# Attention in a two-layer diffusion block: maxima one pair per step, sums by wide matmuls, shift rows by DMA, and one addition moved from GpSimd to VectorE

## The reference

```python
def block_attention(q, k, v, scale):
    ...
    def one_block(qi):
        s = jnp.einsum('bqhgd,bkhd->bhgqk', qi, k, preferred_element_type=F32) * scale
        p = jax.nn.softmax(s, axis=-1).astype(v.dtype)
        return jnp.einsum('bhgqk,bkhv->bqhgv', p, v)
...
def attention_groups(fq, fkv_list):
    ...
    ya = block_attention(fq['aq'].reshape(bsz, t, A_KV_HEADS, A_GROUP, HEAD_DIM), cat('ak'), cat('av'), HEAD_DIM ** -0.5)
    yb = block_attention(fq['bq'][:, :, :, None, :], cat('bk'), cat('bv'), (B_NOPE + B_ROPE) ** -0.5)
```

## Time and profile before

| | |
|---|---|
| median of 3 runs | 4570.11 us (4565.5 to 4571.17) |
| the profiled execution's own time | 4556.52 us |
| its span | 4554.7 us |
| mean granted clock of TensorE | 0.866 |
| PE, DVE, ACT, POOL busy | 85%, 47%, 26%, 18% of the span |
| attention, layer 0: first scores to the last exponential | 939.6 to 1341.6 us |
| attention, layer 1: the same | 3252.3 to 3628.7 us |

### The profile page before, as it was taken

One profiled execution on the slowest core, in us unless ns is written; L12 is line 12 of the kernel. 1 busy time (PEld: TensorE's weight loads), 2 busy tenths in 40 slices (PEclk: granted clock), 3 DMA queues, 4 the chain that ended last, 5 costly groups with the idle time before them and its releaser, 6 DMA issues. The chain is left out here.

```text
span 4554.7 us, 49366 instructions
## 1 busy us (share of the span) xinstructions
PE 3887.8 (85%) x20550; PEld 2092.8 (46%) x20550; DVE 2159.6 (47%) x3601; ACT 1203.1 (26%) x1589; POOL 798.9 (18%) x412
## 2 busy tenths in 40 slices
PE   6698459689989799999996696478799985999996
PEld 6455337323345555555553454455233332444443
DVE  1782886554530623333335683854555316333334
ACT  0321333223331321111112321332233323221211
POOL 0000641056650000000000000700277600000000
PEclk7898665689999799999998897755799997999998
DMA  4210013010002221111101210031100021111110
GB/s 167 54 38 4 1 44 116 17 35 9 1 3 81 74 65 42 42 39 40 42 28 37 56 41 1 1 123 54 30 8 1 1 74 46 51 51 51 51 47 37
DMA packets 207632, 194.37 MB, mean 43 GB/s; under 512 B 9719, under 2 KB 174386, under 8 KB 206770
## 3 DMA queue, kind: packets, MB, share of 16 engines
q1 hardware_dynamic: 203250, 182.84, 12.9%
q10 hardware_dynamic: 4160, 8.39, 0.5%
HBM read 167.48 MB, written 14.68 MB: 40 GB/s over the span
## 5 line engine op out<-in xcount | busy, mean ns | idle before, releaser
L324 PE MATMUL mlp_acc<-hh,mlp_w 128*128 128x512 f16 (+1 forms) x3840 | 752.8, 359 | 49.9 <-DVE mlp_w L314 49.9
L324 PE MATMUL mlp_acc<-mlp_aa,mlp_w 128*128 128x512 f16 (+1 forms) x3840 | 749.2, 358 | 0.0
L324 PEld LDWEIGHTS mlp_acc<-hh,mlp_w 128*128 128x128 f16 x3840 | 376.5, 98 | 424.3 <-DVE mlp_w L314 50.8
L324 PEld LDWEIGHTS mlp_acc<-mlp_aa,mlp_w 128*128 128x128 f16 x3840 | 375.8, 98 | 371.1
L1465 DVE TENSOR_REDUCE at_mx<-at_small 128x1 f32<-128x512 f32 (+1 forms) x600 | 336.5, 591 | 327.8 <-PE at_small L1511 197.1
L1414 POOL TENSOR_TENSOR at_accp<-at_accp,at_p 128x1024 f32<-128x1024 f32 x192 | 450.6, 2347 | 151.7 <-ACT at_p L1445 150.5
L324 PE MATMUL in_acc<-hh,in_w 128*128 128x512 f16 (+1 forms) x2088 | 400.2, 354 | 71.0 <-DVE in_w L314 58.5
L1445 ACT ACTIVATE at_p<-at_sT 128x1024 f32<-128x1024 f32 x246 | 252.1, 1025 | 475.9 <-PE at_sT L1556 458.3
L647 DVE SCALAR_TENSOR_TENSOR yf<-mlp_acc,yf 128x1280 f32<-128x1280 f32 (+1 forms) x112 | 152.0, 1357 | 398.6 <-PE mlp_acc L324 398.6
L324 PEld LDWEIGHTS in_acc<-hh,in_w 128*128 128x128 f16 (+1 forms) x2088 | 208.0, 100 | 261.3 <-DVE in_w L314 59.3
L634 DVE TENSOR_TENSOR mlp_r<-mlp_r 128x1280 f32<-128x1280 f32 (+1 forms) x64 | 86.9, 1358 | 476.2 <-ACT mlp_r L615 476.2
(11 more groups left out here) (268 smaller groups left out, 4870.2 us busy)
## 6 DMA issues: line engine op xcount, KB each, us to landing
mlp_stage<-in_w_ff SPq DMA_DIRECT2D x128, 512.0 KB, 3.9
pa_wada<-in_w_ada SPq DMA_DIRECT2D x16, 2048.0 KB, 8.2
in_stage<-in_w_in SPq DMA_DIRECT2D x36, 512.0 KB, 4.2
set_wada<-in_w_ada ACTq DMA_DIRECT2D x4, 2048.0 KB, 20.2
out_stage<-in_w_out SPq DMA_DIRECT2D x16, 512.0 KB, 5.0
nf_wada<-in_w_ada SPq DMA_DIRECT2D x4, 2048.0 KB, 8.7
x<-x_scratch SPq DMA_DIRECT2D x1, 5120.0 KB, 16.0
xin<-in_x SPq DMA_DIRECT2D x8, 512.0 KB, 6.1
```

Of the source, the lines that this page charges most:

```text
L324: last = self.nc.tensor.matmul(acc[0:mw, a:a + c], w[:, wh, k, m0:m0 + mw], src[:, sh, k0 + k, a:a + c], start=(k == 0 and wh == 0 and sh ...
```

## The change

`max` tasks are streamed, one pair (both heads) in each step, all ahead of `weighted`. The last keys of two query tiles share one task, so that a long unit has 20 tasks of 512 columns. `row` becomes one fp16 matmul that transposes all eight columns of maxima; ACT negates them into a small tile `row`, and SP copies that to the shift rows by DMA. `sum` becomes two fp32 matmuls of 64 x 512 columns with a matrix of ones, so that the sums are already spread; ACT copies them to `o32`, DVE takes the reciprocals in four pieces of 128 columns in four steps, and `bc` is gone. POOL leaves out steps 4 and 5 of a long unit; DVE adds these two to `accd`, and POOL adds `accd` in one operation. `p32` has five buffers instead of four.

```diff
-EARLY = 2
-PRING = 4
+PRING = 5
+LEAD = 4
+DVE_PAIR = (4, 5)
...
     def maxes(u):
-        return [("max", u, par, q, c) for q in range(4) for c in range(len(units[u].keys)) for par in range(2)]
+        if not units[u].long:
+            return [("max", u, par, 0, (q, q + 1)) for q in (0, 2) for par in range(2)]
+        whole = [("max", u, par, c, (q,)) for q in range(4) for c in range(2) for par in range(2)]
+        return whole + [("max", u, par, 2, (q, q + 1)) for q in (0, 2) for par in range(2)]
...
+        for n in range(len(both) - 1, -1, -1):
+            u, k = both[n]
+            when[n] = min(base[u] - LEAD, when.get(n + 1, N) - (1 if n + 1 < len(both) else 0))
+        for n, (u, k) in enumerate(both):
+            want.setdefault(max(when[n], n // 2), []).extend(maxes(u)[2 * k:2 * k + 2])
+        for u in range(1, U):
+            want.setdefault(base[u] - LEAD + 1, []).append(("row", u))
...
+            sum_at[u] = min(end + (3 if soon else 4), N)
+            for k in range(4):
+                piece_at.setdefault(min(end + (4 if soon else 5 + k), N), []).append((u, k))
+            scale_at[u] = min(end + (4 if soon else 9), N)
...
# SP
+                for pr in range(QRING):
+                    load(pr)
+                for u in range(U):
+                    sp.wait_ge(s_row, u + 1)
+                    for par in range(2):
+                        for pr, tok, c, n in units[u].parts:
+                            r = 4 * par + c // P
+                            dst = shift_row(pr, par)[:, tok:tok + n]
+                            sp.dma_start(dst, row[r:r + n // P, u % 2, :]).then_inc(s_shift[u % 2], 16)
...
# POOL
+                            if joins[i]:
+                                pool.wait_ge(s_dacc, adds_d[i])
+                                other = accd[:, :, :]
...
# ACT
+                            nc.scalar.activation(row[:, u % 2, :], sm[j % 2][0:8, 0:P], ACT.Copy, scale=-1.0).then_inc(s_row, 1)
+                            nc.scalar.activation(o32[:, u % 2, :], sm[j % 2][:, :], ACT.Copy).then_inc(s_sums, 1)
...
# DVE
+                        part = o32[:, u % 2, k * P:(k + 1) * P]
+                        pieces[u] = ch(nc.vector.reciprocal(part, part))
...
                 for i in range(N):
+                    if joins[i]:
+                        dve.wait_ge(s_p, i + 1)
+                        nc.vector.tensor_tensor(accd[:, :, :], p32[:, (i - 1) % PRING, :, :], p32[:, i % PRING, :, :],
+                                                ALU.add).then_inc(s_dacc, 1)
                     tasks(i)
+                    scale(i)
...
# PE
+                            last = nc.tensor.matmul(out[0:8, 0:P], top[:, u, :], ident[:, :], start=True, stop=True)
+                            for par in range(2):
+                                last = nc.tensor.matmul(out[64 * par:64 * par + 64, :], e.ones[:, 0:64],
+                                                        accp[:, u % 2, par, :], start=True, stop=True)
...
                     scores(i)
-                    tasks(i, slice(0, EARLY))
+                    tasks(i, ahead)
                     if i >= LAG:
                         weighted(i - LAG)
-                    tasks(i, slice(EARLY, None))
+                    tasks(i, ("sum",))
```

More of the change, by code:

```diff
@@ L850, in mixers @@
         attention(nc, e, sem, l, f)
-MSHIFT = 8.3178
 def halves(t, a, n):
@@ L1242, in attention @@
     last_use = {pr: max(u for u in range(U) if pr in [p[0] for p in units[u].parts]) for pr in range(6)}
-    adds = []
+    adds, joins = [], []
     for u, s in steps:
-        adds.append(0 if s == 0 else 1)
+        adds.append(0 if s == 0 or (units[u].long and s == DVE_PAIR[0]) else 1)
+        joins.append(units[u].long and s == DVE_PAIR[1])
     adds_p = [sum(adds[:i + 1]) for i in range(N)]
+    adds_d = [sum(joins[:i + 1]) for i in range(N)]
     def consumed(eng, i):
         u, s = steps[i]
-        eng.wait_ge(s_pacc, adds_p[base[u] + max(s, 1)])
+        if units[u].long and s in DVE_PAIR:
+            eng.wait_ge(s_dacc, adds_d[base[u] + DVE_PAIR[1]])
+        else:
+            eng.wait_ge(s_pacc, adds_p[base[u] + max(s, 1)])
     small, at = [], {}
@@ L1324, in attention, with shifts @@
                 last_max[t[1]] = kinds[:j + 1].count("max")
-            elif t[0] == "row":
-                rows_at[j] = sum(len(units[w[1]].parts) for w in small[:j + 1] if w[0] == "row")
-                rows_through[t[1]] = rows_at[j]
+        def shifts(u):
+            return sum(16 * 2 * len(units[v].parts) for v in range(u % 2, u + 1, 2))
         def hi_of(t, q):
@@ L1482, in tasks, with scale @@
+                pieces = {}
+                def scale(i):
+                    for u, k in piece_at.get(i, []):
+                        part = o32[:, u % 2, k * P:(k + 1) * P]
+                        dve.wait_ge(s_sums, u + 1)
+                        pieces[u] = ch(nc.vector.reciprocal(part, part))
+                    for u in range(U):
+                        if scale_at[u] == i:
                             dve.wait_ge(s_pv, base[u + 1])
+                            ch.wait(dve, pieces[u])
@@ new lines, in tasks @@
+                            for n, q in enumerate(tiles):
+                                pr, tok = units[u].tile(q)
+                                if pr < 4 and pr % 2 == 0 and pr not in loaded:
+                                    pe.wait_ge(s_kload[pr // 2], 16 * 6)
+                                    loaded.add(pr)
+                                if pr < 4:
+                                    R = slice(64 * par, 64 * par + 64)
+                                    query, key = hi_of(f.aq[R, pr, :], tok), kk[R, pr // 2, a:a + w]
+                                else:
+                                    b = 2 * (pr - 4) + par
+                                    query, key = f.qb[0:96, 0, b, tok:tok + P], f.kb[0:96, 0, b, a:a + w]
+                                last = nc.tensor.matmul(out[:, n * w:(n + 1) * w], query, key, start=True, stop=True)
+                        elif kind == "row":
+                            pe.wait_ge(s_top, u + 1)
+                            if u == 0:
+                                pe.wait_ge(s_id, 1)
+                            last = nc.tensor.matmul(out[0:8, 0:P], top[:, u, :], ident[:, :], start=True, stop=True)
+                        else:
@@ L1546, in scores @@
                     if s == 0:
-                        pe.wait_ge(s_row, rows_through[u])
+                        pe.wait_ge(s_shift[u % 2], shifts(u))
+                        for pr, _, _, _ in units[u].parts:
+                            if pr < 4 and (pr, "q") not in loaded:
+                                pe.wait_ge(s_load[pr % QRING], per_pair * (pr // QRING + 1))
+                                loaded.add((pr, "q"))
                     if i >= 2:
```

149 lines of the change are left out of this document (54 added, 95 removed).

## The result

| | before | after |
|---|---|---|
| median of 4 runs each | 4570.64 us (4565.5 to 4576.94) | 4492.82 us (4491.55 to 4494.73) |
| profiled execution's own time | 4556.52 us | 4493.94 us |
| a clean grouped-query unit | 29.2 us | 26.40 us |
| a latent unit | 33.2 us | 30.8 us |
| units 1 to 7 of layer 1 | 218.0 us | 185.6 us |

What follows compares the result with a forecast made beforehand. PE's order of work was taken as the bound. Unit gains of 27, 11, 4 and about 1, minus 8.6, plus 1, minus 1 gave 34 us less; with 6 from the clock, 40 less, forecast 4530, own range 4500 to 4560.

Steps and rivals of the forecast that it cites:

- PE's order as the path: In attention, PE goes from scores to maxima to weighted sum without a break, so its order of work sets the time.
- the sum without stalls: PE's work in a changed grouped-query unit: 24.3 us against 29.2, so 4.9 us less before stalls.
- The two stalls: PE waits for DVE at step 6's maxima, 1.55 us, and at step 7's row matmul, 1.5 us; latent units 0.8 and 1.0.
- my list: DVE's work from step 5, in series: addition, step 5's reductions, reciprocal, step 6's reductions, top maxima, reciprocal, ended at 7.25 us.
- The clock: Falls of the granted clock cost about 25 us in both layers; a quarter, 6 us, was forecast to come back.
- The start of layer 0: Shift rows are issued behind SP's loads of three head pairs, so the first scores come late: 8.6 us lost.
- The addition as a loss: DVE's addition ahead of step 5's reductions gains nothing and costs the 1.55 us stall in a grouped-query unit.
- GpSimd not the bound: POOL's additions were not the bound before the change, 22.0 us of a 29 us unit.
- The rival that the reciprocal shares it with GpSimd: Each reciprocal waits 1 us on average for POOL's port: 80 us more, 46 slower in all, 4616; chance 0.13.
- the small operations: Among the work DVE loses by the change, listed beside the copy and four reductions' overhead, with no size given.
- the case without stalls: Rival: DVE's queue catches up before PE asks, 87 us less, about 4480; chance 0.08.

Runs made afterwards that it cites:

- e8: Changed kernel with all ten steps added on GpSimd, row task behind the weighted sum, and unit 0's shift rows ahead of the third pair's loads: 4438.0 us.
- e1: Changed kernel with the addition back on GpSimd for all ten steps and none on VectorE: 4466.1 us.
- e2: Changed kernel with the shift row's matmul behind the weighted sum of its step instead of ahead of it: 4483.7 us.
- e5: Kernel before, with only the wide sums, ScalarE's copy and VectorE's four reciprocals, and no broadcast: 4515.8 us.
- e3: Changed kernel with eight one-column matmuls of the old sum put ahead of the wide sum, their result overwritten: 4556.9 us.
- e9: Changed kernel with VectorE's addition behind step 5's two reductions instead of ahead of them: 4479.2 us.
- e4: Changed kernel with SP issuing unit 0's shift rows before it loads the third head pair: 4479.2 us.
- e11: Kernel before with wide sums and streamed maxima, plus the negation on ScalarE instead of VectorE and the constant left out: 4480.2 us.
- e7: Kernel before with both wide sums and streamed maxima, keeping the old row tasks: 4523.7 us.
- e12: Kernel before with only the negation moved to ScalarE and the constant left out: 4563.7 us.

## Why the prediction was right, and where its sizes were off

**PE's order as the path: right.** An ordinary step is 2.31 us, as computed from the starts in the earlier trace rows. e8, with every wait gone, is at 24.1 against the 24.3 of the sum without stalls.

**The two stalls: right in place, too long in size.** In a long unit behind the first of its layer PE waits for DVE in step 6 and at the row in step 7, and nowhere else. Removing the addition (e1) takes the first away and moving the row (e2) takes the second away, so both causes are shown. But they are 1.33 and 0.98 us, not 1.55 and 1.5, and the sum costs 0.86, not 1.0. What failed is how I laid out DVE's work: I set each instruction behind the whole duration of the last. In the trace the next one starts sooner. The addition is listed with 1.23 us, and the reductions start 1.15 after it; a reciprocal is listed with 0.94 and in a full queue takes 0.86 from start to start. Over the six entries of my list ahead of the row (two of them pairs of reductions) that is 0.6 us. A grouped-query unit takes 26.4 instead of 27.3 us, a latent one 30.8 instead of 31.3: 14 x 0.9 + 6 x 0.5 = 16 us.

**The clock: the largest error.** I had given back a quarter of the loss, 6 us, since two idle stretches were to take the place of the thin one. All of it came back in the grouped-query units. In layer 1 the seven units gain 32.4 us, of which 7 x 2.8 = 19.6 are the clean units, and 12.8 the clock. Over both layers attention, from SP's first load to the last low half, takes 72.2 us less (441.8 to 412.7, and 413.5 to 370.3). My own terms with the measured sizes (39.2 + 14.4 + 4 - 8.3 + 2 - 1, of which the 4 and the 1 are the forecast's own and were not measured) give 50. So some 22 us are the clock's, by difference; only the 12.8 of layer 1 are read directly. e5 shows that the wide sum, with the broadcast gone, is enough for this, and e3 that one thin stretch brings falls back. That an idle wait could do the same was not wrong in itself: in e9 a fall followed a wait of 1.23 us in two units. The waits of the long units after the change are up to 0.9 us, and no fall follows them. Behind the first two short units of layer 0, whose four reciprocals stand in one step, PE waits 3.24 and 2.49 us. The prediction had put this stall at 4 us and counted nothing for these units. A fall follows both; at the first the matmuls take 1.95 us instead of 1.08, and the granted clock from 1085.10 to 1088.50 is 0.51:

```profile
1085.08 1.95 PE L1601 MATMUL at_acc<-at_p,av 128*64 128x512 f32 x4 [3.24 <-DVE at_o L1517]
```

**The start of layer 0: right**, 8.3 us lost for 8.6, and e4 gets them back by order alone. Layer 1's start gained 2.0 for 1.

**The addition as a loss, and GpSimd not the bound: right**; e1 measures 21 to 27 us. The prediction's 1.55 in each of 14 units and 0.8 in six is 26.5.

**The port.** The rival that the reciprocal shares it with GpSimd is refuted: all 108 take between 0.89 and 0.95 us, with GpSimd busy beside 76 of them. The addition never waits either, 1.224 to 1.227 us: GpSimd was idle beside each of the 24, as the prediction's timeline had it. The shared port was there in another place that I did not look at: the negation of the maxima, which the change moved to ScalarE. I had counted that among "the small operations" at nothing. The step that failed is that DVE's small operations were weighed by their number and not by their listed time; L1471 in before takes 1.18 us on average, for eight columns. By e11 and e7 its removal is worth 1.32 us a unit once the sums are wide and the maxima streamed, and by e12 nothing in before. The Trainium skill (SBUF — State Buffer, Who interferes with whom) says that a tensor_scalar can run in a two-port mode, and that beside a GpSimd instruction the one that was issued later is then blocked for the whole of the other. The trace agrees: 25 of the 27 in before started while a GpSimd addition ran, and each of them ended 0.03 us behind that addition's end; the other two met an idle GpSimd and took 0.17 us.

**What the parts are worth** in a grouped-query unit, one on top of the other: 29.2 before, 27.4 with wide sums (and the clock back), 27.85 with streamed maxima, 26.5 with the negation on ScalarE, 24.9 with the row as one matmul and a DMA (e1, which also has the fifth buffer of `p32`), 26.4 with the addition on VectorE. The streaming gains nothing until the negation is moved; with it, 0.9 us (e5 to e11), although the row task is still the costly one. What the last step to e1 owes to the row, the DMA and the fifth buffer was not taken apart.

**The numbers.** Forecast 4530, measured 4492.8: 7 us outside of the forecast's own range (4500 to 4560), and 0.8 us inside the wide one (4492 to 4585), which is luck, since stages that no edit touches move by more. The mechanism was right and the gain was almost twice the forecast's. Of the 37 us, 16 are the clock, 16 the stalls and the sum, and 1 the starts. The rest is not attention's: outside of it the trace of after is 10 us longer than before's, and before's profiled execution lay 14 us under its median. No single rival came true; the case without stalls (about 4480) came nearest in time for the wrong reason. Moved by 0.6 us, neither stall would have changed the sign.

## What to carry to other kernels

When a queue is followed, take the distances between starts in a full queue, not the listed durations. In a fixed order, a place can decide more than the cost of the task: look at what stands right behind the moved work, and at what it used to cover. A tiny instruction with a long listed time may be a wait, as it was here, and is worth a line of the sum.

## What the runs showed of the hardware

A VectorE tensor_scalar on 8 columns took between 0.17 and 2.21 us (e7, L1488, 27 of them). The 25 that started while a GpSimd addition ran ended 0.03 us behind the end of that addition, whenever they had started. A reciprocal of 128 columns beside GpSimd's additions did not wait (0.95 us at most, after, L1512).

The granted clock fell after one-column fp32 matmuls (e3, 1.95 us of them, in some units and not in others), and after plain idle time too (3.24 us behind a short unit of after, and 1.23 in e9). In e9 PE was idle for 1.23 us ahead of a row matmul, and the scores from 997.85 on take 0.63 us instead of 0.38; that unit lasts 27.26 us at 0.94. The same wait in the other units of e9 but one cost no clock.

```profile
996.34 0.22 PE L1565 MATMUL at_small<-at_ident,at_top 128*8 128x128 f16 x1 [1.23 <-DVE at_mx L1498]
...
997.85 0.63 PE L1589 MATMUL at_sT<-at_qs,at_ks 65*128 65x512 f16 x1
```

Stages that the change does not touch move, by some 10 us, and so by as much as the 0.2% that the forecast took for the measurement. From 700 to 800 us, ahead of attention, both kernels run the same part of the program, and the windows of before show a granted clock of 0.57,

```profile
700.00:800.00 100.00, 99.90 (x407) 80.60 (x406) 64.10 (x104) 39.92 (x74) 9.79 (x9) 0.57 0.27 95
```

those of after 0.52, with a tenth fewer matmuls done:

```profile
700.00:800.00 100.00, 100.00 (x367) 79.93 (x367) 60.92 (x98) 37.07 (x69) 9.05 (x8) 0.52 0.26 90
```

Attention then starts 8.3 us later (SP's first load at 922.41 instead of 914.13). e1 and e8 show 0.53 and 0.52 there, e4 0.57 again; e1 and e4 ran on one chip, so it is not the chip alone. What sets it was not found.
